# A LayerNorm mean summed on other engines, wider convolution groups, and idle products in waits: a hybrid encoder step on one core

## What is computed

```python
def conv_module(h, buf, w_pw1, b_pw1, w_dw, b_dw, ln_g, ln_b, w_pw2, b_pw2):
    u = h @ w_pw1 + b_pw1
    a, gt = jnp.split(u, 2, axis=-1)
    glu = a * jax.nn.sigmoid(gt)
    xp = jnp.concatenate([buf, glu], axis=1)     # 30 rows of history ahead
    y = causal_dwconv(xp, w_dw, b_dw)            # 31 taps, each channel by itself
    y = jax.nn.silu(layernorm(y, ln_g, ln_b))    # mean and variance over 1024 channels
    return y @ w_pw2 + b_pw2, new_buf
...
def trunk(x, ...):
    for i in range(DEPTH):
        x = x + (conv_module if i == 0 else hgrn2_mix)(rmsnorm(x), ...)
        x = x + conv_ffn(rmsnorm(x), ...)
    return rmsnorm(x)
```

## Time and profile before

| | |
|---|---|
| time, three runs | 2886.12, 2890.53, 2891.44 us; median 2890.53 |
| the profiled execution | 2888.88 us, its span 2887.10 us |
| mean granted clock of TensorE | 0.986 of full |
| busy: TensorE, its weight loads | 2849.4 us (99%), 2798.9 us (97%) |
| busy: VectorE, ScalarE, GpSimd | 1662.5 us (58%), 529.3 us (18%), 834.4 us (29%) |
| chain that ended last | TensorE 89%, VectorE 9% |
| stage the change touches | up to about 382 us of the span |

### The profile page before, as it was taken

The page is one execution under the profiler, slowest core; times in us unless marked ns, Lnnn a source line. Parts: engine busy times, 40 slices in busy tenths (PEclk is TensorE's granted clock), DMA queues, the critical chain, the costliest instruction groups (busy, mean ns, idle before and its releaser), DMA issues.

```text
span 2887.1 us, 40334 instructions
## 1 busy us (share of the span) xinstructions
PE 2849.4 (99%) x16832; PEld 2798.9 (97%) x16832; DVE 1662.5 (58%) x1821; ACT 529.3 (18%) x647; POOL 834.4 (29%) x686
## 2 busy tenths in 40 slices
PE   8999999999999999999999999999999999999998
PEld 8999799999999999999999999989999999999998
DVE  8995336454545455466676667781744555454445
ACT  3001323111111111231111111121311111111122
POOL 5221154222222222243121222114322222222224
PEclk9999599999999999999999999999999999999999
DMA  5223021111111111121111110103111111111112
GB/s 152 57 59 57 0 109 44 38 43 44 44 38 41 44 44 40 41 108 52 46 45 38 45 46 31 47 30 116 38 43 44 44 39 41 44 44 39 41 45 79
DMA packets 109012, 147.07 MB, mean 51 GB/s; under 512 B 65265, under 2 KB 78065, under 8 KB 108913
## 3 DMA queue, kind: packets, MB, share of 16 engines
q1 hardware_dynamic: 48624, 112.48, 12.3%
q10 hardware_dynamic: 60288, 33.14, 4.0%
HBM read 129.13 MB, written 16.47 MB: 50 GB/s over the span
## 4 chain that ended last, share of the span: by engine, by line
PE 89%; DVE 9%; issue 1%; ACT 1%; POOL 0%; DMA 0%; DVEq 0%; ACTq 0%; POOLq 0%
PE BANKS L649 63%; PE BANKS L895 11%; PE BANKS L937 3%; PE BANKS L1123 3%; DVE BANKS L1678 1%; PE BANKS L722 1%; PE BANKS L720 1%; PE BANKS L857 1%; DVE HGA L2032 1%; DVE HGA L1997 1%; DVE HGA L2019 1%; PE BANKS L745 1%; DVE XL L1590 1%; PE BANKS L986 1%; DVE X L1678 1%
## 5 line engine op out<-in xcount | busy, mean ns | idle before, releaser
L535 POOL TENSOR_TENSOR SMALL<-WRAW 128x1 f32<-128x1 f32 x196 | 48.4, 247 | 1916.3 <-PE BANKS L649 1334.1
L649 PE MATMUL BANKS<-XH,WH 128*128 128x384 f32 x2592 | 592.0, 336 | 0.6 <-DVE X L1603 0.5
L649 PE MATMUL BANKS<-XL,WH 128*128 128x384 f32 x2592 | 588.6, 334 | 0.0
L649 PE MATMUL BANKS<-XH,WL 128*128 128x384 f32 x2592 | 588.6, 334 | 0.0
L538 POOL TENSOR_TENSOR WL<-WRAW,WH 128x1024 fp32r<-128x1024 f32 x196 | 476.5, 2431 | 15.7
L649 PEld LDWEIGHTS BANKS<-XL,WH 128*128 128x128 f32 x2592 | 462.2, 188 | 0.0
L649 PEld LDWEIGHTS BANKS<-XH,WL 128*128 128x128 f32 x2592 | 462.1, 188 | 0.0
L649 PEld LDWEIGHTS BANKS<-XH,WH 128*128 128x128 f32 x2592 | 460.4, 188 | 1.7 <-DVE X L1603 0.9
L1815 DVE TENSOR_TENSOR X<-BANKS,X 128x1152 f32<-128x1152 f32 x168 | 228.0, 1357 | 267.4 <-PE BANKS L649 206.4
L1872 DVE SCALAR_TENSOR_TENSOR ARENA<-ARENA 128x1168 f32<-128x1168 f32 x176 | 255.7, 1453 | 130.9 <-ACT ARENA L1377 122.2
L1377 ACT ACTIVATE ARENA<-ARENA 128x1168 f32<-128x1168 f32 x88 | 120.3, 1367 | 943.7 <-DVE ARENA L1612 943.7
(11 more groups left out here) (214 smaller groups left out, 3474.7 us busy)
## 6 DMA issues: line engine op xcount, KB each, us to landing
WRAW<-in_w SPq DMA_DIRECT2D x188, 512.0 KB, 3.5
X<-in_x SPq DMA_DIRECT2D x8, 576.0 KB, 9.0
X<-in_x ACTq DMA_DIRECT2D x8, 576.0 KB, 7.2
x_kept<-X ACTq DMA_DIRECT2D x8, 576.0 KB, 2.8
X<-x_kept ACTq DMA_DIRECT2D x8, 576.0 KB, 7.4
HGA<-taps_padded ACTq DMA_DIRECT2D x32, 128.0 KB, 3.5
HGA<-in_state ACTq DMA_DIRECT2D x8, 512.0 KB, 4.3
out_hgs<-HGA ACTq DMA_DIRECT2D x8, 512.0 KB, 2.6
```

What stands on the lines that cost most here:

```text
L535: nc.gpsimd.tensor_tensor(PAD, one, one, ALU.mult)
L649: ins = nc.tensor.matmul(ps_bank(n, c), w, x[:, third(c)], start=(k == 0 and q == 0), stop=(k == last and q == 2), skip_group_check=betwee ...
```

## The change

1. A new buffer MSUM (in GLU buffer 2, which is free by then) takes the sum of tiles 0 to 5: ScalarE writes tile 0 plus BSUM (`first_of_sum`, ahead of the sigmoid of tile 7), GpSimd adds tiles 1 to 5, after the split of the last value unit's weights. TensorE's mean is then three products of MSUM, three of tile 6 (between the groups of tile 7) and three of tile 7.
2. GpSimd's splits of U_PW2 and U_PW2 + 1 now come after these sums and after the last transpose of `forward` (xt_rdy).
3. Every convolution instruction takes the 40 columns of its group up to three times (a dimension with step 0), as far as the bank has room: 120 columns for 28 of 32 groups, 80 for two, 40 for two. The further copies fall on places of later groups, which overwrite them, or on unused ones.
4. `variance` and `fin_sum` multiply by 128 columns of ones, where it was one; the roots read every 128th column.
5. TensorE has idle products (256 columns, the result unused): 8 ahead of tile 7's groups, 6 ahead of the last mean products, 2 after them, 2, 1 and 3 in the normalisation.

```diff
+        EARLY = KD - 2
+        MSUM = GLUS[2][:, 0:T]
...
             for u in range(3, U_PW2):
                 split(u)
+            for k in range(1, EARLY):
+                pool.wait_ge(msum, k)
+                if k in TOEPLITZ:
+                    pool.wait_ge(bt_free, TOEPLITZ.index(k) + 1)
+                    pool.wait_ge(str_rdy, TOEPLITZ.index(k) + 1)
+                else:
+                    pool.wait_ge(taps_done, len([c for c in range(k + 1) if c not in TOEPLITZ]))
+                nc.gpsimd.tensor_tensor(MSUM, MSUM, X[:, k, :], ALU.add).then_inc(msum, 1)
+            pool.wait_ge(xt_rdy, len(TOEPLITZ))
             split(U_PW2)
             split(U_PW2 + 1)
...
-                    out = PS[:, n % 2 * NCH + g // BANK_GROUPS, at:at + COLS]
-                    nc.tensor.matmul(out, WT[:, g, 0, :], XT[0][:, :, g], start=True, stop=False, ...)
-                    ins = nc.tensor.matmul(out, WT[:, g, 1, :], XT[1][:, :, g], start=False, stop=True, ...)
+                    times = min(3, (512 - at) // COLS)
+                    out = PS[:, n % 2 * NCH + g // BANK_GROUPS, at:at + times * COLS].rearrange(
+                        "p (r b) -> p r b", r=times)
+                    for t in range(2):
+                        blocks_of = XT[t][:, :, g].rearrange("p (r b) -> p r b", r=1).broadcast_to([P, times, COLS])
+                        ins = nc.tensor.matmul(out, WT[:, g, t, :], blocks_of, start=t == 0, stop=t == 1, ...)
...
-                ins = nc.tensor.matmul(ps_bank(T_MEAN, c), NEG_MEAN, X[:, k, third(c)], start=False, ...)
+                ins = nc.tensor.matmul(ps_bank(T_MEAN, c), NEG_MEAN, (MSUM if k < EARLY else X[:, k, :])[:, third(c)],
+                                       start=k < EARLY, ...)
...
+            def idle_products(times, out):
+                for _ in range(times):
+                    nc.tensor.matmul(out[:, 0:2 * P], IDENT, CONST[:, 0:2 * P], start=True, stop=True)
             free_slot(T_MEAN)
-            pe.wait_ge(mg_rdy, 1)
             for c in range(NCH):
-                nc.tensor.matmul(ps_bank(T_MEAN, c), NEG_MEAN, BSUM.broadcast_to([P, CW]), start=True, ...)
-            parts = [(k, c) for k in range(KD - 1) for c in range(NCH)]
-            ahead = len(parts) - (BLK // 2 - 2)
-            for k, c in parts[:ahead]:
-                mean(k, c)
-            for g in range(0, BLK, 2):
-                convolved(KD - 1, g, g + 2)
-                if g // 2 < len(parts) - ahead:
-                    mean(*parts[ahead + g // 2])
+                mean(0, c)
+            idle_products(8, MB[:, 0, :])
+            for g in range(0, BLK, 4):
+                convolved(KD - 1, g, g + 4)
+                if BLK // 2 <= g < BLK // 2 + 4 * NCH:
+                    mean(KD - 2, g // 4 - BLK // 8)
+            idle_products(6, MB[:, 0, :])
             for c in range(NCH):
                 mean(KD - 1, c)
+            idle_products(2, MB[:, 0, :])
...
-                        ins = nc.tensor.matmul(ps_bank(T_VAR, c)[:, t:t + 1],
-                                               LSQ[:, KD * c + 2 * p, t * P:(t + 1) * P], ONES[:, 0:1],
+                        ins = nc.tensor.matmul(ps_bank(T_VAR, c)[:, t * P:(t + 1) * P],
+                                               LSQ[:, KD * c + 2 * p, t * P:(t + 1) * P], ONES,
...
             variance(2)
+            free_slot(T_PW2)
+            idle_products(2, ps_bank(T_PW2, 2))
             spread_norm(1)
+            idle_products(1, ps_bank(T_PW2, 2))
             spread_norm(2)
+            idle_products(3, ps_bank(T_PW2, 2))
...
+            def first_of_sum():
+                act.wait_ge(mg_rdy, 1)
+                act.wait_ge(taps_done, 1)
+                act.wait_ge(glu_free[2], 2)
+                act.wait_ge(cache_out[2], 64)
+                A(MSUM, X[:, 0, :], ACT.Identity, bias=BSUM).then_inc(msum, 1)
...
             history_in(7)
+            first_of_sum()
             sigmoid(7)
```

More of the change, by code:

```diff
@@ L366, in build @@
         pair_rdy = sem("pair_rdy")
+        msum = sem("msum")
         mean_full, stmp_rdy, ln_out, ln_hi_pool = sem("mean_full"), sem("stmp_rdy"), sem("ln_out"), sem("ln_hi_pool")
@@ L718, in convolved @@
                     at = g % BANK_GROUPS * COLS
-                    out = PS[:, n % 2 * NCH + g // BANK_GROUPS, at:at + COLS]
[L720 to L723, removed]
+                    times = min(3, (512 - at) // COLS)
[3 more added lines that the diff above has]
+                        blocks_of = XT[t][:, :, g].rearrange("p (r b) -> p r b", r=1).broadcast_to([P, times, COLS])
+                        ins = nc.tensor.matmul(out, WT[:, g, t, :], blocks_of, start=t == 0, stop=t == 1,
+                                               skip_group_check=True)
                 if c == KD - 1:
@@ L738, in mean @@
             def mean(k, c):
-                if c == 0 and k in TOEPLITZ:
+                if c == 0 and k < EARLY:
+                    pe.wait_ge(msum, EARLY)
+                elif c == 0:
                     pe.wait_ge(bt_free, TOEPLITZ.index(k) + 1)
                     pe.wait_ge(str_rdy, TOEPLITZ.index(k) + 1)
[L743 to L746, removed]
+                ins = nc.tensor.matmul(ps_bank(T_MEAN, c), NEG_MEAN, (MSUM if k < EARLY else X[:, k, :])[:, third(c)],
+                                       start=k < EARLY, stop=k == KD - 1, skip_group_check=True)
                 if k == KD - 1:
@@ L795, in _ @@
                 big(pw1_tile("V", c), U_PW1 + 2 * c + 1, between=with_conv(c - 1) if c - 1 in TOEPLITZ else None)
+            def idle_products(times, out):
+                for _ in range(times):
+                    nc.tensor.matmul(out[:, 0:2 * P], IDENT, CONST[:, 0:2 * P], start=True, stop=True)
             free_slot(T_MEAN)
-            pe.wait_ge(mg_rdy, 1)
             for c in range(NCH):
-                nc.tensor.matmul(ps_bank(T_MEAN, c), NEG_MEAN, BSUM.broadcast_to([P, CW]), start=True, stop=False,
-                                 skip_group_check=True)
-            parts = [(k, c) for k in range(KD - 1) for c in range(NCH)]
-            ahead = len(parts) - (BLK // 2 - 2)
-            for k, c in parts[:ahead]:
-                mean(k, c)
-            for g in range(0, BLK, 2):
-                convolved(KD - 1, g, g + 2)
-                if g // 2 < len(parts) - ahead:
-                    mean(*parts[ahead + g // 2])
+                mean(0, c)
[5 more added lines that the diff above has]
+            idle_products(6, MB[:, 0, :])
             for c in range(NCH):
                 mean(KD - 1, c)
+            idle_products(2, MB[:, 0, :])
             def variance(c):
@@ L1162, in fin_sum @@
                         a = c * CW + t * P
-                        ins = nc.tensor.matmul(MB[:, c % 2, t:t + 1], squares[:, a:a + P], ONES[:, 0:1],
+                        ins = nc.tensor.matmul(MB[:, c % 2, t * P:(t + 1) * P], squares[:, a:a + P], ONES,
                                                start=squares is ACC and t == 0,
@@ L1333, in ln_root @@
                 act.wait_ge(var_full, c + 1)
-                A(R9[:, c * NCH:(c + 1) * NCH], ps_bank(T_VAR, c)[:, 0:NCH], ACT.Sqrt, bias=EPSC, scale=1.0 / D
+                A(R9[:, c * NCH:(c + 1) * NCH], ps_bank(T_VAR, c)[:, 0:CW:P], ACT.Sqrt, bias=EPSC, scale=1.0 / D
                   ).then_inc(root_rdy, 1)
@@ L1552, in _ @@
                 act.wait_ge(fin_sums, c + 1)
-                A(R9[:, c * NCH:(c + 1) * NCH], MB[:, c % 2, 0:NCH], ACT.Sqrt, bias=EPSC, scale=1.0 / D
+                A(R9[:, c * NCH:(c + 1) * NCH], MB[:, c % 2, 0:CW:P], ACT.Sqrt, bias=EPSC, scale=1.0 / D
                   ).then_inc(fin_root, 1)
```

1 line of the change is left out of this document (removed).

## The result

The changed kernel takes 2909.8 us (median of 2908.59 to 2910.82) against 2890.8 for the kernel before on the same chip: a ratio of 1.0067, 95% interval 1.0051 to 1.0083. It is slower by 0.67%; the forecast was 2874 us, and rival 2 (half rate for strided columns, 2906 us) is the nearest. The profiled execution took 2910.82 us, 21.9 us more than that of before.

The account below looks back on a forecast made before the run. TensorE was taken as the bound, busy almost all the time, its clock and instruction costs deciding. Gains of -33.4 us and +18.5 for strided columns gave -14.9: 2888.9 to 2874 us, range 2852 to 2906.

Parts of the forecast that it names:

- rival 2: Convolution groups: strided columns come at half rate, 1.67 ns each, +50.5 us in all, 2906 us; chance 0.22.
- (h): 120-column groups in five convolutions: 1.2 ns a strided column, 145 ns an instruction for 112, +3.7 us each, +18.5 us.
- (a): Tile 7's groups and the mean: full clock and three mean products in place of 14, 43.3 to 16.2 us, -27.0 us.
- (b): Start of tile 7: transposes end sooner and the last taps' DMAs land sooner, -1.7 us (bounds 0 and -2.4).
- (c): From tile 7's last group to VectorE's first centring: 4.1 us becomes 3.4, -0.7 us.
- (d): Normalisation: third variance at full clock takes 2.7 us, not 5.12; -2.0 us (bounds -3 and +1).
- (e): Half-clock stretch from 249.74 us, after 40-column groups: goes if 120 columns hold the clock, -1.7 us.
- (f): The end of the kernel: the same one-to-128-column change, VectorE bound there, -0.3 us.
- (g): Work moved to ScalarE and GpSimd (mean sum, two weight splits): fits in their waits, 0 us.
- Rival 3: Tile 7: the clock stays at half because strided groups after the gap don't bring it back, 2890 us; chance 0.08.

Follow-up runs that it names:

- in_unit_40: The changed kernel with 120 columns only in tile 7's groups, the groups inside value units having 40 again: 2866.7 us, ratio 0.9917.
- step_1: The changed kernel with convolution columns read side by side, not 128 bytes apart (wrong columns, five convolutions not computed): 2857.6 us, ratio 0.9881.
- by_group_7: The changed kernel with 40 columns inside units and tile 7's operand written group by group, so its columns are contiguous: 2859.2 us, ratio 0.9892.
- steps: The changed kernel with column distances of 8, 12, 16, 32, 4 bytes in tiles 1, 3, 5, 6, 7 (convolutions not computed): one execution, 2884.6 us.
- group_40: by_group_7 with 40 contiguous columns in tile 7's groups in place of 120, idle products kept: 2872.2 us, ratio 0.9948.
- mean_only: The changed kernel with 40 columns in every group and no idle products; shorter mean, moved splits and 128-column variances stay: 2871.8 us, ratio 0.9946.
- variance_1: by_group_7 with the variances of the convolution module's LayerNorm on one column of ones again, idle products kept: 2862.7 us, ratio 0.9893.
- no_idle: by_group_7 without its 22 idle products: 2859.4 us, ratio 0.9883.

## Why the prediction was wrong

The step that failed is (h), "the groups of 120 columns". It said +3.7 us a convolution, +18.5 in all, with 1.2 ns a strided column. The runs showed 11.0 in each of the four units (in_unit_40) and 9.2 in tile 7 (27.3 against 18.1 in step_1 and by_group_7): 53.2 us. The mechanism was named, and was rival 2; its size was off by a factor of three, and the upper bound I gave the step, 180 ns an instruction, lay under the 206 measured.

Why the rows misled: I took (296 - 250)/39 from the earlier trace rows as the time of a column. But durations in a run don't grow by a column's time. In step_1 120 contiguous columns last 275 ns; one column lasts 250 in the kernel before: 0.2 ns a column, while 384 contiguous columns start every 0.323 us, 0.84 ns a column: the plain rate. What a row in a run does show is the excess over a contiguous operand of like width. (The ends of matmuls are modelled in these profiles.) Groups of 120 columns, after and in step_1 (ns min/median/max):

```profile
L741 PE MATMUL BANKS<-HGA x360: 229/383/432, 85.6 to 263.6; 128*128 128x120 f32 x156, 128*128 128x80 f32 x12, 128*128 128x40 f32 x12
```

```profile
L742 PE MATMUL BANKS<-HGA x128: 241/275/427, 281.4 to 299.2; 128*128 128x120 f32 x112, 128*128 128x80 f32 x8, 128*128 128x40 f32 x8
```

(383 - 275)/120 = 0.90 ns beyond the plain 0.84: 1.74, beside the measured 1.72. The medians of steps, 330, 392 and 398 ns at 12, 16 and 32 bytes, give 1.30, 1.82 and 1.87 in the same way, beside the measured 1.33, 1.78 and 1.82. Something near it could have been read from the earlier trace rows: (296 - 262)/40 = 0.85, beside the contiguous row of 16 columns, plus 0.84 is 1.69 ns, an instruction of 0.203 us and a sum of 2907. I left the plain rate out of the quotient. The same quotient at half clock, (414 - 352)/39 = 1.6, is no rate either: 384 contiguous columns take 0.71 us there, 1.85 ns a column. That no excess is seen at half clock was right all the same: in group_40 forty contiguous columns last 414 ns too.

I also held half the rate unlikely because of the 1.2, and weighed too little: ScalarE's 1.8 ns a column at the same 128 bytes was the nearest row of a long strided access. And I priced (h) as a tax on the whole change, without asking what 120 columns could give inside the units: by the earlier trace rows the clock was full there but for 3.4 us. That comparison, 3.7 us of cost each against nothing to gain, would have condemned the edit in four of five places at my own price.

The other steps, each as it came out:

| step | forecast | measured |
|---|---|---|
| (a) tile 7 and mean, without (h) | -27.0 | -25.2 (43.3 to 18.1 in step_1; one half-clock stretch at its start) |
| (b) start of tile 7 | -1.7 | -1.4 |
| (c) last group to centring | -0.7 | -0.7 |
| (d) normalisation | -2.0 | -1.3 (clock 0.54 from 371.0 to 374.4; the third variance takes 4.3 us, not 2.7) |
| (e) half-clock stretch at 249.74 | -1.7 | -2.3 (273.15 against 275.43) |
| (f) the end | -0.3 | -0.4 |
| (g) moved work | 0 | 0 |
| (h) strided columns | +18.5 | +53.2 |

Without (h) the forecast was -33.4, the sum of the measured ones is -31.3, and step_1 is 31.4 us under the kernel before in the profiled executions. With (h), 2888.9 - 31.3 + 53.2 = 2910.8, the profiled time.

(b) came for the reason given. The GLU step ahead of the transposes was quick, as the earlier trace rows had it for a step beside no split, GpSimd's split waited, and with no weight load behind them the last taps landed sooner, 3.2 us after their issue in place of 5.2 (timelines of VectorE and GpSimd, after; DMAs issued from 321.85 to 322, to landing):

```profile
318.98 1.29 DVE L1690 SCALAR_TENSOR_TENSOR HGA<-HGA,PAR,X 128x1024 f32<-128x1024 f32 x1
```

```profile
323.74 0.19 POOL L539 TENSOR_TENSOR SMALL<-WRAW 128x1 f32<-128x1 f32 x1 [31.86 <-DVE HGA L1729]
```

```profile
HGA<-taps_padded ACTq DMA_DIRECT2D x2, 128.0 KB, 3.2
```

(e) has the right size and the wrong reason. The stretch at 249.74 is also absent in the nine kernels above whose units have 40 columns, so 120 columns did not remove it. All nine have the shorter mean and the moved splits; what of it matters was not tried, and stays open.

Rival 3 was half right in its reason: 40-column groups after the gap do stay at half clock (mean_only, group_40), but 120 columns, strided or not, bring it up.

## What to carry to other kernels

Before widening an operand to keep TensorE's clock up, look at how far apart its elements lie: in these runs, at float32 and 16 bytes or more, each column costs 1.7 to 1.8 ns, which 40 columns hide behind the weight load (starts 0.112 us apart) and 120 don't. Widen it only where the clock is really down, and lay the data out contiguously first, here with a transpose that had to write it anyway (2.1 us more of VectorE, 0.6 of them felt). Price an unknown operand by its excess over the like contiguous one plus the plain rate, and take a change in several places apart, place by place: here four of five places could only lose.

## What the runs showed of the hardware

- A strided moving operand of TensorE in float32, 120 columns, full clock: 0.112 us at 4 and 8 bytes, 0.160 at 12, 0.213 at 16, 0.218 at 32; 0.206 at 128 bytes with 40 columns read three times. At half clock the last takes 0.213, the pace of the weight loads: the full clock is worth 3% to it.
- Width, not layout, set the clock of tile 7: 40 columns half (with one or two idle products of 256 columns after four groups too), 80 half and then full, 120 full but for 3 to 6 us at the start.
- Variances of 128 columns of ones did not keep the clock up all through either, but shortened the half clock: 7 us in by_group_7, where one column had 17 (variance_1); in the changed kernel it was 3.4 us, where the kernel before had 17.1.
- Kernels whose tile 7 has 40 columns vary with that clock: group_40 from 2871.3 to 2889.0 us at mean clocks of 0.993 to 0.987, the kernel before once 2867.8 at 0.994 in 13 executions. With 120 columns the times lie within 2 us in by_group_7 and no_idle and within 5 us in in_unit_40, but those are four executions each, against ten and thirteen.
